# Second layer's attention in pairs of jobs: normalised before the turn, values as the stationary operand, two banks for each of three stages

## What is computed

```python
# 12 query heads on 4 key/value heads, head width 64, window 128, sinks; plus 4 heads over 256 memory tokens
s = einsum('bnqhgd,bnkhd->bnhgqk', qb, kband) * 64 ** -0.5      # blocks of 128 queries x 256 keys (the first: 128)
s = where(valid, s, -inf)
m = maximum(max(s, -1), sink)
p = exp(s - m);  p = p / (sum(p, -1) + exp(sink - m))
o = einsum('bnhgqk,bnkhd->bnqhgd', p, vband)
# memory heads: p = softmax(q mk^T * 64 ** -0.5);  mo = p @ mv
mix = concatenate([o, mo], -1) @ w_out[1]                        # 512x1024 times 1024x1024
x = x + rmsnorm(mix, g_mix_post[1])
```

## Time and profile before

| | |
|---|---|
| median of 3 runs | 2076.01 us (2075.76 to 2080.66) |
| profiled execution | 2072.65 us, its span 2071.2 us |
| PE busy | 2003.9 us, 97% of the span |
| DVE, ACT, POOL busy | 1176.7 (57%), 929.6 (45%), 229.0 us (11%) |
| chain that ended last | PE 81%, DVE 12%, ACT 6%, issue 1% |
| mean granted TensorE clock | 0.997 |

### The profile page before, as it was taken

One profiled execution on the slowest core, in us unless ns is written; L12 is line 12 of the kernel. 1 busy time (PEld: TensorE's weight loads), 2 busy tenths in 40 slices (PEclk: granted clock), 3 DMA queues, 4 the chain that ended last, 5 costly groups with the idle time before them and its releaser, 6 DMA issues.

```text
span 2071.2 us, 25475 instructions
## 1 busy us (share of the span) xinstructions
PE 2003.9 (97%) x10032; PEld 1663.2 (80%) x10032; DVE 1176.7 (57%) x2622; ACT 929.6 (45%) x1926; POOL 229.0 (11%) x185
## 2 busy tenths in 40 slices
PE   7999999999999999999999999999999999999998
PEld 7987788888887777788888888878767887877787
DVE  4526464433226677463444226998976638867744
ACT  5547454433124477453343223367744233356631
POOL 1001010000001000000000002576730100000000
PEclk9999999999999999999999999999999999999999
DMA  5420122223233222222222233222222222210131
GB/s 201 159 86 37 62 92 84 99 102 102 97 107 116 78 89 86 92 92 102 102 95 88 102 105 117 85 82 82 82 92 102 102 97 74 95 41 21 41 122 61
DMA packets 29511, 190.07 MB, mean 92 GB/s; under 512 B 3456, under 2 KB 3728, under 8 KB 8144
## 3 DMA queue, kind: packets, MB, share of 16 engines
q1 hardware_dynamic: 25696, 175.98, 24.5%
q0 software_dynamic: 2544, 10.37, 1.5%
q10 hardware_dynamic: 1152, 2.10, 0.3%
HBM read 184.24 MB, written 4.19 MB: 91 GB/s over the span
## 4 chain that ended last, share of the span: by engine, by line
PE 81%; DVE 12%; ACT 6%; issue 1%; DMA 0%; SPq 0%; DVEq 0%; ACTq 0%
PE bank L432 23%; PE bank L433 23%; PE bank L434 23%; DVE bank L2251 5%; PE bank L1913 2%; PE bank L1901 1%; PE bank L588 1%; ACT WH L375 1%; PE bank L1293 1%; DVE WL L399 1%; PE bank L1906 1%; PE bank L1800 1%; DVE WL L404 1%; PE bank L1391 1%; PE bank L1278 1%
## 5 line engine op out<-in xcount | busy, mean ns | idle before, releaser
L432 PE MATMUL bank<-XH,WH 128*128 128x512 f32 (+2 forms) x1504 | 587.8, 391 | 7.8 <-DVE WL L399 3.8
L434 PE MATMUL bank<-XH,WL 128*128 128x512 f32 (+2 forms) x1504 | 559.8, 372 | 0.0
L433 PE MATMUL bank<-XL,WH 128*128 128x512 f32 (+2 forms) x1504 | 559.3, 372 | 0.0
L432 PEld LDWEIGHTS bank<-XH,WH 128*128 128x128 f32 (+1 forms) x1504 | 281.9, 187 | 68.9 <-issue 14.2
L433 PEld LDWEIGHTS bank<-XL,WH 128*128 128x128 f32 (+1 forms) x1504 | 282.0, 188 | 53.1 <-issue 6.0
L434 PEld LDWEIGHTS bank<-XH,WL 128*128 128x128 f32 (+1 forms) x1504 | 281.5, 187 | 50.3
L404 DVE TENSOR_TENSOR WL<-RAW,WH 128x2048 fp32r<-128x2048 f32 x60 | 137.5, 2291 | 285.6 <-ACT WH L378 285.6
L378 ACT ACTIVATE WH<-RAW 128x2048 fp32r<-128x2048 f32 x81 | 154.8, 1911 | 265.4 <-PE bank L434 265.4
L399 DVE SCALAR_TENSOR_TENSOR WL<-RAW,cols,WH 128x256 fp32r<-128x256 f32 (+2 forms) x456 | 201.5, 511 | 80.7 <-ACT WH L375 80.6
L375 ACT ACTIVATE WH<-RAW,cols 128x256 fp32r<-128x256 f32 (+2 forms) x456 | 200.8, 522 | 41.4 <-PE bank L434 34.0
L2251 DVE SCALAR_TENSOR_TENSOR bank<-conv_in,cols,bank 128x512 f32<-128x512 f32 x290 | 198.1, 747 | 1.1
(11 more groups left out here) (324 smaller groups left out, 3091.4 us busy)
## 6 DMA issues: line engine op xcount, KB each, us to landing
RAW<-weights SPq DMA_DIRECT2D x164, 1024.0 KB, 4.8
row_a<-rows POOLq DMA_DIRECT2D x6, 512.0 KB, 4.8
x_res<-x SPq DMA_DIRECT2D x4, 512.0 KB, 10.8
kv<-mem_park POOLq DMA_DIRECT2D x2, 1024.0 KB, 5.1
out<-x_res ACTq DMA_DIRECT2D x8, 256.0 KB, 2.1
mem_tok<-mem SPq DMA_DIRECT2D x1, 1024.0 KB, 6.9
mem_tok<-mem POOLq DMA_DIRECT2D x1, 1024.0 KB, 5.2
mem_park<-m_keys POOLq DMA_DIRECT2D x2, 512.0 KB, 2.9
```

The source lines that it names most:

```text
L432: pe.matmul(ps, ah, bh, start=first, stop=False)
L433: pe.matmul(ps, ah, bl, start=False, stop=False)
L434: return pe.matmul(ps, al, bh, start=False, stop=last)
```

## The change

Jobs go in pairs: pair p is the jobs 2p and 2p+1, 32 pairs, 8 of memory and 24 of the window. For each pair:

- both scores lie side by side in one `S` buffer; their banks are a ring of two (`"scores"`, banks 2 and 3). The negative maximum, sink term, sum and reciprocal are now one instruction for both jobs.
- DVE multiplies the probabilities by the reciprocal (`slide_scaled_dve`, two instructions a pair) before the turn.
- one bank of two (`"turned"`) takes the pair's transposes, and one ACT copy moves them to `T`.
- the values stay in the array as the stationary operand, 64 columns of it a job, and `T` moves with 128 columns. The result comes out transposed: job 2p in partitions 0 to 63, job 2p+1 in 64 to 127 of one bank of two (`"values"`).
- ACT copies it to `mixed_high` (128x128), DVE makes its low part in `XL`. So `mixed`, its scaling and `turn_mixed` in all three engines are gone.

The stages follow in fixed lags of steps: on PE turn of n-2, scores of n, values of n-3; on ACT high part of n-4, copy of the turn of n-2, exponentials of n, then the side work; on DVE low part of n-4, normalisation of n-1, maximum of n, then the side work, then rotation. Both side lags are 1, and the quarters stand in neighbouring entries. The product's tiles 0 to 2 of the first unit are issued in the three steps after the last pair; tile 3 and the second unit follow.

```diff
+    "scores": (2, 2), "turned": (4, 2), "values": (6, 2)          (rings in take_bank)
-    SLIDE_ORDER = staggered(16 + len(SWA), (0, 2, 3, 5))
-    EARLY_BLOCKS, LATE_BLOCKS, LATE_STEP = (0, 1, 2, 3, 6, 7), (4, 5), 15
+    PAIRS = 8 + len(SWA) // 2
+    TURN_LAG, VALUE_LAG, PART_LAG = 2, 3, 4
+    SLIDE_STEPS = PAIRS + PART_LAG
+    EARLY_BLOCKS, LATE_BLOCKS, LATE_STEP = (0, 1, 2, 3, 6, 7), (4, 5), 8
-                QUARTERS[e + 1 + 2 * q] = q
-    BESIDE_LAGS = 2, 3
+                QUARTERS[e + 1 + q] = q
+    BESIDE_LAGS = 1, 1
+        for n in range(SLIDE_STEPS):                               # PE
+            step = [(stage, n - lag) for stage, lag in ((1, TURN_LAG), (0, 0), (2, VALUE_LAG)) if 0 <= n - lag < PAIRS]
...
+            if n >= PAIRS and n < PAIRS + 3:
+                out_tile_pe(n - PAIRS, 0)
+    def slide_values_pe(p):
+        PE.wait_ge(*after("emptied", "slide_turn", p))
+        ps = take_bank("values", "slide_out", p)
+        n = slide_width(p) // P
+        for c in range(n):
+            for i in range(2):
+                mm = pe.matmul(ps[HD * i:HD * i + HD, 0:P], slide_value(2 * p + i, c),
+                               T_buf[p % 4][:, (n * i + c) * P:(n * i + c + 1) * P], start=c == 0, stop=c == n - 1)
+        for n in range(SLIDE_STEPS + BESIDE_LAGS[1]):              # ACT
+            if n == LATE_STEP:
+                turn_all_act("qT", LATE_BLOCKS, qT)
+            if 0 <= n - PART_LAG < PAIRS:
+                slide_high_act(n - PART_LAG)
+            if 0 <= n - TURN_LAG < PAIRS:
+                slide_turn_act(n - TURN_LAG)
+            if n < PAIRS:
+                slide_exp_act(n)
             for other in beside(n, BESIDE_LAGS[0]):
                 beside_act(other)
+    def slide_scaled_dve(p):
+        if p < 8:
+            DVE.wait_ge(*after("emptied", "mem", 1, 2 * p + 1))
+        else:
+            DVE.wait_ge(*after("slide_exp", p))
+            dve.tensor_tensor(stat_pair(2, p), stat_pair(2, p), stat_pair(3, p), ALU.add).then_inc(*V.mark())
+            DVE.wait_ge(*V.so_far())
+        dve.reciprocal(stat_pair(4, p), stat_pair(2, p)).then_inc(*V.mark())
+        DVE.wait_ge(*V.so_far())
+        for i in range(2 * p, 2 * p + 2):
+            S = slide_scores_of(i)
+            dve.tensor_scalar(S, S, stat(4, i), None, ALU.mult)...
+        for n in range(SLIDE_STEPS + BESIDE_LAGS[1]):              # DVE
+            if 0 <= n - PART_LAG < PAIRS:
+                slide_low_dve(n - PART_LAG)
+            if 0 <= n - 1 < PAIRS:
+                slide_scaled_dve(n - 1)
+            if n < PAIRS:
+                slide_max_dve(n)
             for other in beside(n, BESIDE_LAGS[1]):
                 beside_dve(other)
+            if 1 <= n <= NT:
+                rotate_dve(q_tok, SH - KB, ("q", 1), KB, ("q", 1), range(n - 1, n), LATE_BLOCKS[0])
```

More of the change, by code:

```diff
@@ L328, in take_bank @@
     def take_bank(ring, *group):
-        first, count = {"product": (0, 4), "spare": (4, 4), "all": (0, 8), "beside": (0, 2), "six": (2, 6), "five": (3, 5), "third": (2, 1), "fourth": (3, 1), "jobs": (6, 2), "sums": (7, 1)}[ring]
+        first, count = {"product": (0, 4), "spare": (4, 4), "all": (0, 8), "beside": (0, 2), "six": (2, 6), "five": (3, 5), "third": (2, 1), "fourth": (3, 1), "jobs": (6, 2), "sums": (7, 1), "scores": (2, 2), "turned": (4, 2), "values": (6, 2)}[ring]
         b = first + turn.get(ring, 0) % count
@@ L498, in from_x, with from_mixed @@
         return XH, XL, kb
+    def from_mixed(kb):
+        return mixed_high, XL, kb
     def from_y(kb):
@@ L1454, in mlstm_pool, with out_tile_pe, out_first_pe @@
         head_norm_pool()
[L1458 to L1462, removed]
-            for t in range(NT):
[L1464 to L1477, removed]
-    LATE_TILE = [(0, 1), (1, 1), (3, 0), (2, 1), (3, 1)]
[L1482 to L1485, removed]
-            chunk_pe(U["out", layer, 0], ("out", layer, 0), 512, KB, NT, from_x)
+    LATE_TILE = [(0, 1), (1, 1), (3, 0), (2, 1), (3, 1)]
+    def out_tile_pe(t, b):
+        if t == 0:
+            PE.wait_ge("split_lo", U["out", 1, b] + 1)
+        PE.wait_ge(*after("emptied", "slide_out", last_pair(t)))
+        chunk_tile_pe(U["out", 1, b], ("out", 1, 0), t, 4 * b, 512, KB, from_mixed,
+                      ring=("beside", "beside", "third", "fourth")[t], last=t == NT - 1)
+    def out_first_pe(layer):
+        if layer:
+            out_tile_pe(3, 0)
+            for t in range(NT):
+                out_tile_pe(t, 1)
         else:
@@ L1805, in slide_scores_pe @@
     def slide_scores_pe(i):
         if i < 16:
-            memory_job_pe(0, i, i, 1, lambda c: qT[:, 6 + c, :], "six")
+            memory_job_pe(0, i, i, 1, lambda c: qT[:, 6 + c, :], "scores")
             return
@@ L1814, in slide_scores_pe, with slide_turn_act @@
             PE.wait_ge(*after("emptied", "qT", LATE_BLOCKS[-1]))
-        ps = take_bank("six", "swa", i - 16)
+        ps = take_bank("scores", "swa", i - 16)
         pe.matmul(ps[:, 0:w], qT[r, h // 2, t * P:(t + 1) * P], keys[r, g // 2, (t + 1) * P - w:(t + 1) * P],
                   start=True, stop=True).then_inc(*T.mark("full", "swa", i - 16))
+    def slide_turn_act(p):
+        w = 2 * slide_width(p)
+        ACT.wait_ge(*after("full", "slide_turn", p))
+        act.activation(T_buf[p % 4][:, 0:w], bank_of("slide_turn", p)[:, 0:w], AF.Copy).then_inc(
+            *A.mark("emptied", "slide_turn", p))
@@ new lines, in slide_low_dve @@
+    def slide_low_dve(p):
+        kb, tt = pair_place(p)
+        DVE.wait_ge(*after("high", "slide_out", p))
+        dve.tensor_tensor(XL[:, kb, tt], bank_of("slide_out", p)[:, 0:P], mixed_high[:, kb, tt].bitcast(F32),
+                          ALU.subtract).then_inc(*V.mark("emptied", "slide_out", p))
+    def sliding_dve():
+        for n in range(SLIDE_STEPS + BESIDE_LAGS[1]):
[5 more added lines that the diff above has]
+                slide_max_dve(n)
```

149 lines of the change are left out of this document (78 added, 71 removed).

## The result

The changed kernel takes 2100.36 us (median of 4 runs, 2099.06 to 2102.45), the kernel before on the same chip 2075.89 (2074.70 to 2080.66). The ratio is 1.0117, with an interval of 1.0105 to 1.0129. The forecast was 2100; +23.9 us were forecast, the medians differ by 24.5.

A forecast was written before the change was run, and what follows sets the result against it. It took a DVE-ACT loop of 3.86 us a pair, plus quarters, to bound the stage. The first 96 product matmuls would end at 888.0 instead of 864.1: 2076.0 + 23.9 = 2100 us, range 2092 to 2108.

The forecast's parts named there:

- ACT's and DVE's quarters: Weights' side work on the link: a step with k quarters costs 0.35 + 0.60k us more; 36 quarters in 16 steps.
- rival 1: PE stays the stage's bound, link under 3.5 us, quarters hidden, gain at the end kept: 2067 us; chance 0.08.
- Memory pairs: Pairs 0 to 7, where PE's 3.4 us a pair decides; with quarters, rotations and late query blocks 36.8 us.
- the next six: Pairs 8 to 14: 6 x 3.22, seven quarters 5.3, first wide one 0.5, together 25.1 us.
- the last seventeen: Pairs 14 to 31: 17 x 3.86, 17 quarters 13.0, copies 2.0, together 80.6 us.
- The link: DVE-ACT loop per pair of 256 keys: maximum, exponentials, high part, low part, sum, reciprocal, scalings, 3.86 us.
- Values: PE's eight value matmuls for two jobs and 256 keys: 0.84 us, up to 1.7 without overlap or hidden loads.
- The end: From pair 31's exponential at 863.7 through the product's first 96 matmuls, with turn and values, to 888.0.
- the sign of the clock: 128x512 matmuls of the product's first tiles more than 0.23 us apart would show the clock at work.
- Rival 3 (the clock): PE's long waits lower its clock, overrunning the link by up to 3 us: +10 to +15, 2110 to 2115; chance 0.07.
- gap of 3.6 us at step 17: PE's longest wait in the stage, at the step with four quarters: 3.86 + 2.75 + 0.5 less 3.5.
- Rivals 1 and 2: Rival 2: link near 3.5 us, the stage grows by what the end gives, 2070 to 2082; chance 0.07.

The follow-up runs named there:

- experiments 2 to 6: Changed kernel, DVE's side work later 2094.08 us; low part later 2093.74; both 2069.28; both plus normalisation later 2073.22; needless DVE instruction on loop 2112.00, off it 2100.44.
- 7: Changed kernel with four banks for scores, one for turned probabilities and one for values: 2101.84 us.
- 8: Changed kernel plus one to three needless PE matmuls ahead of the turn in eleven pairs whose steps have quarters: 2101.32 us.
- Experiment 1: Changed kernel with DVE normalising the pair two back instead of one back, turn, values and parts one step later: 2106.36 us.
- experiment 3: Changed kernel with DVE making the low part of the pair five back instead of four back: 2093.74 us.
- experiment 4: Changed kernel with DVE's low part one step later and DVE's side work two steps behind PE instead of one: 2069.28 us.
- experiment 9: Kernel with both DVE shifts (low part and side work later), the values' two loops swapped so neighbouring matmuls use the same column half: 2071.70 us.

## Why the prediction was right, and where it was not

**Direction and cause: right.** A loop between DVE and ACT bounds the stage and not an engine's busy time (experiments 2 to 6); banks (7) and clock (8) don't. ACT's and DVE's quarters lie on it, at 4.66 us for one (0.97 over a link without, forecast 0.95) and 6.13 for three (2.44, of which a key copy is a part; forecast 2.15).

**Which instruction closes the loop: wrong.** The prediction wrote that DVE's maximum of n+1 stands behind the normalisation of n, and that only a maximum ahead of the normalisation would spare it (rival 1). Experiment 1 did away with that order and gained nothing. The working had the right term all the same: "it waits for this, not for the exponentials alone", of the low part. The step that failed is the inference from a sum of terms to the one that could be spared. Moving the low part made the links without quarters 3.34 (experiment 3), and moving DVE's quarters as well brought 2069 (experiment 4), where rival 1 said 2067, with the normalisation left where it was.

**Terms that were off and cancelled.** Times of the profile after, less 3.07. The first exponential: 721.4, forecast 721.2. From there ACT's timeline has the first pair, pairs 8, 14 and 31 at:

```profile
724.43 0.47 ACT L1860 ACTIVATE S<-bank,small 128x256 f32<-128x256 f32 x1 [1.03 <-DVE small L1896]
...
760.41 0.40 ACT L1863 ACTIVATE S<-S,small 128x128 f32<-128x128 f32 x1 [1.29 <-DVE small L1900]
...
784.72 0.51 ACT L1863 ACTIVATE S<-S,small 128x256 f32<-128x256 f32 x1 [2.55 <-DVE small L1900]
...
863.77 0.51 ACT L1863 ACTIVATE S<-S,small 128x256 f32<-128x256 f32 x1 [2.31 <-DVE small L1900]
```

- Memory pairs 36.0 us, forecast 36.8; the next six 24.3, forecast 25.1; the last seventeen 79.05, forecast 80.6. Together 3.2 us less. The link was 3.69 and not 3.86. By the timelines above: the maximum to ACT 1.19 (forecast 1.22), ACT to DVE's low part 1.38 (1.52; two exponentials 0.50 each, and the sink's lets the next start after 0.09 and not 0.18), low part 0.21, sum 0.18, reciprocal 0.20, scaling 0.53 (0.54).
- Values: 0.59 us in place of 0.84 for two jobs, and two times 0.47 before. It lay off the path. The Trainium skill (TensorEngine Tiling, Key Properties) says that a change of tiling mode drains TensorE. The prediction would have added 0.1 to 0.2 us a pair for it; no run shows that price. The 0.59 runs to the start of the full-array matmul behind the eight, so whatever the change of mode costs is in it, and it is less than the 0.89 of eight on the whole array. PE was busy for 83% of the stage, forecast 75 to 80.
- The end took 2.5 us more, from pair 31's exponential to the last of 96 matmuls (890.6; 26.8 against 24.3). Not seen in the forecast: the first product tiles use the banks of the side work, which ACT empties a step later. PE's timeline:

```profile
865.58 0.47 PE L436 MATMUL bank<-WH,mixed_high 128*128 128x512 f32 x1 [1.53 <-ACT m_values L1742]
...
870.22 0.50 PE L436 MATMUL bank<-WH,mixed_high 128*128 128x512 f32 x1 [0.59 <-ACT m_values L1742]
...
875.32 0.39 PE L436 MATMUL bank<-WH,mixed_high 128*128 128x512 f32 x1
...
876.02 0.39 PE L436 MATMUL bank<-WH,mixed_high 128*128 128x512 f32 x1
```

  These two waits are 2.1 us. Three matmuls then take 0.70, so 0.233 each, where the earlier trace rows gave 21.75 / 96 = 0.227; over 96 that is 0.6. The forecast had named this, more than 0.23 apart, as the sign of the clock. The sign was wrong: the granted clock is 1.00 there. All variants have this spacing too (0.233 to 0.235 on average), and 0.226 to 0.227 right ahead of the stage, so it belongs to the product as changed; the cause is open.
- The start 0.2 later, the pairs 3.2 less, the end 2.5 more: 887.5 against a forecast of 888.0. That the sum came out right to a microsecond is luck to the extent of those 3 us; the range of 2092 to 2108 is what the working could bear.

**Rival 3 (the clock)** was right in that the clock fell, at three places of the four or five looked for, and wrong in its price: it took PE's slow work to overrun the link by up to 3 us each time, and the one overrun that can be read cost 1.1 us. Its gap of 3.6 us at step 17 didn't come either: in that link of 6.95 us PE was busy for 5.60, and its longest wait was 0.88. The Trainium skill (TensorE: Matmul & The Clock Gate, Why this matters for your kernels) advises against idle gaps over about 3 us between bursts of matmuls. In this stage no wait of PE's matmuls reached 3 us, and the clock still fell, with waits of 2.89, 1.62 and 2.38 us ahead, so keeping under that figure was not enough here. **Rivals 1 and 2** didn't occur.

## What to carry to other kernels

Engines that take their work in order can form a loop even where no data goes round: an instruction for an old job that stands ahead of a new one's makes the new one wait for everything that stood ahead of its own input on the other engine. So before a pipeline's lags are fixed, go through what each cross-engine wait is really a wait for (the other engine's whole queue of that step), and put any step whose input is produced at the tail of the other engine's step one step later; here two such shifts were worth 31 us together and 6 each alone, while a third, of the instruction that the forecast took for the cause, made the kernel slower. Where two loops stand side by side, taking the longer one away shows only the difference to the next. A needless instruction put once on and once off the suspected loop tells with two kernels whether the loop is the bound.

## What the runs showed of the hardware

- Eight f32 matmuls with weights of 128x64 and 128 columns moving take 0.59 us, 0.074 each, while eight with full 128x128 weights take 0.89, 0.111 each. The time doesn't depend on whether neighbours use different column halves (experiment 9). Which of the two, smaller weight loads or overlap, gives it the runs don't tell.
- PE was granted the lower level of its clock in three stretches of 7, 7 and 4 us, with waits of 2.89, 1.62 and 2.38 us just ahead. In experiment 1 a wait of 2.40 brought no fall. A slow stretch cost between nothing and 1.1 us where the loop between DVE and ACT bound the stage.
- The 128x512 matmuls of the product's first half start 0.227 us apart before and 0.233 after, at a granted clock of 1.00 in both. The cause is open.
